# The first microseconds of a decoder-layer kernel: token loads, turns and the first two projection tiles in two token parts

## The reference, cut to what matters

```
z = h @ w_in                                    # h: 544 tokens x 1024, w_in: 1024 x 1696
q_lat, kv_lat, k_rope, lru_x, lru_gate = split(z)
xc, new_buf = causal_conv(lru_x, ...)           # width 4, depthwise
y, hT = rg_lru(xc, h0, lp)                      # sigmoid gates, exp, sqrt, a scan over tokens
mem_kv: m = rmsnorm(mem) ; k = m @ w_mem_k ; v = m @ w_mem_v     # 256 memory rows
```

## Time and profile before

| | |
|---|---|
| time, 3 runs | 1021.93, 1022.85, 1022.96 us; median 1022.85 |
| profiled execution, span from first to last instruction | 1026.9 us (no other time of that execution is given) |
| PE busy | 995.7 us, 97% |
| DVE, ACT, POOL busy | 518.6, 298.6, 447.6 us |
| chain that ended last | PE 82%, DVE 10%, POOL 3%, ACT 2% |
| mean granted TensorE clock | 0.989 |

### The profile page before, as it was taken

How to read it: one execution, slowest core, us unless ns; L and a number is a source line. 1 busy time by engine, 2 the same in 40 slices (tenths; PEclk the granted TensorE clock), 3 DMA queues, 4 the chain that set the end, 5 groups by cost and what they waited for, 6 DMA issues and landing times.

```text
span 1026.9 us, 19819 instructions
## 1 busy us (share of the span) xinstructions
PE 995.7 (97%) x8511; PEld 899.8 (88%) x8511; DVE 518.6 (51%) x731; ACT 298.6 (29%) x598; POOL 447.6 (44%) x284
## 2 busy tenths in 40 slices
PE   6999999998999999999999999999999999999998
PEld 5989898765677777999965799999999999999997
DVE  5789998478555555564155266421341134114413
ACT  6334265465444443121045122210120022002222
POOL 4545688500011112455320155555555555555551
PEclk8999999998999999999999999999999999999999
DMA  8323355514267772732193022233223322332222
GB/s 232 80 66 83 103 172 160 160 48 185 114 265 278 278 284 75 274 89 82 51 404 101 22 83 83 82 97 89 82 83 95 91 84 82 93 92 83 83 82 87
DMA packets 140556, 130.39 MB, mean 127 GB/s; under 512 B 13477, under 2 KB 133170, under 8 KB 136630
## 3 DMA queue, kind: packets, MB, share of 16 engines
q1 hardware_dynamic: 134888, 88.55, 28.6%
q0 software_dynamic: 2304, 37.75, 9.5%
q10 hardware_dynamic: 3278, 2.83, 0.8%
HBM read 123.53 MB, written 5.03 MB: 125 GB/s over the span
## 4 chain that ended last, share of the span: by engine, by line
PE 82%; DVE 10%; POOL 3%; ACT 2%; issue 2%; DMA 1%; ACTq 1%; SPq 0%; DVEq 0%; POOLq 0%
PE gps L582 56%; PE gps L942 5%; PE aux L956 3%; PE aux L983 3%; POOL wlo L521 2%; PE gps L1098 1%; PE gps L1180 1%; PE aux L962 1%; PE aux L894 1%; PE gps L1018 1%; DVE act_lo L1698 1%; PE gps L718 1%; PE aux L1111 1%; PE aux L973 1%; DVE lt L1782 1%
## 5 line engine op out<-in xcount | busy, mean ns | idle before, releaser
L582 PE MATMUL gps<-act_hi,whi 128*128 128x272 f32 x912 | 266.5, 292 | 5.7 <-POOL wlo L511 3.2
L497 POOL TENSOR_SCALAR whi<-wraw 128x1024 fp32r<-128x1024 f32 (+1 forms) x109 | 114.7, 1052 | 360.1 <-PE gps L582 300.0
L582 PE MATMUL gps<-act_lo,whi 128*128 128x272 f32 x912 | 265.0, 291 | 0.0
L582 PE MATMUL gps<-act_hi,wlo 128*128 128x272 f32 x912 | 264.6, 290 | 0.0
L500 POOL TENSOR_TENSOR wlo<-wraw,whi 128x1024 fp32r<-128x1024 f32 (+1 forms) x109 | 257.7, 2364 | 9.1
L582 PE MATMUL gps<-h_hi,whi 128*128 128x272 f32 x640 | 185.7, 290 | 0.0
L582 PE MATMUL gps<-h_lo,whi 128*128 128x272 f32 x640 | 185.1, 289 | 0.0
L582 PE MATMUL gps<-h_hi,wlo 128*128 128x272 f32 x640 | 184.6, 288 | 0.0
L582 PEld LDWEIGHTS gps<-act_hi,whi 128*128 128x128 f32 x912 | 173.2, 190 | 6.7 <-issue 3.7
L582 PEld LDWEIGHTS gps<-act_hi,wlo 128*128 128x128 f32 x912 | 173.1, 190 | 0.3 <-issue 0.2
L582 PEld LDWEIGHTS gps<-act_lo,whi 128*128 128x128 f32 x912 | 173.0, 190 | 0.0
(11 more groups left out here) (374 smaller groups left out, 1537.6 us busy)
## 6 DMA issues: line engine op xcount, KB each, us to landing
wraw<-in_w_up_dram SPq DMA_DIRECT2D x32, 512.0 KB, 4.0
wraw<-in_w_down_dram SPq DMA_DIRECT2D x32, 512.0 KB, 3.7
wraw<-in_w_in_dram SPq DMA_DIRECT2D x14, 512.0 KB, 4.2
kv<-in_cache_mem_k_dram SPq DMA_DIRECT2D x7, 1024.0 KB, 6.8
kv<-in_cache_mem_v_dram SPq DMA_DIRECT2D x7, 1024.0 KB, 14.0
wraw<-in_w_mem_k_dram SPq DMA_DIRECT2D x16, 256.0 KB, 2.9
wraw<-in_w_mem_v_dram SPq DMA_DIRECT2D x16, 256.0 KB, 3.3
wraw<-in_w_out_dram SPq DMA_DIRECT2D x8, 512.0 KB, 4.6
```

Of the source, the lines that this page charges most:

```text
L497: nc.gpsimd.tensor_scalar(whi[:, slot, 0:n], wraw[:, slot, 0:n], 1.0, 1.0, ALU.mult, ALU.mult).then_inc(pool_step, 1)
L582: mm = nc.tensor.matmul(out_of(a), w_of(w, k), x_of(x, k, part), start=(k == 0 and s == 0), stop=(k == k_tiles - 1 and s == 2))
```

## The change

- The tokens' loads and the weight units' are issued in another order: tokens 0 to 255, unit 0, tokens 256 to 511, the sample tokens, unit 1.
- Projection tiles 0 and 1 use token parts of 256 and 288 columns in place of 272 and 272, and are computed part by part: PE turns tokens 0 to 255, computes half of part 0 of tile 0, turns tokens 256 to 383, computes the other half, turns the rest, and so on. `act_hi` and `act_lo` are made in 8 + 8 instructions in place of 8 each.
- ACT makes `act_hi` of both parts before the squares of the token rows 128 to 543; before, the squares of rows 128 to 255 stood ahead of `act_hi`. A square root of one column at the very start loads its table.
- `dg` is made by DVE (two instructions) in place of POOL (five); the ones-matmul for the factors stands late in tile 1.
- PE turns the memory rows after tile 2 in place of after tile 1.

```
@@ sync
+            load_tokens(0)
+            load_tokens(1)
+            load_unit(0, win_v[:, :, IN_COLS[0]:IN_COLS[0] + 128], 1024)
+            load_tokens(2)
+            load_tokens(3)
+            sp.dma_start(xs[0:TS, 4, :], x_sample.rearrange("b t n -> (b t) n")).then_inc(x_in[4], 16)
+            load_unit(1, win_v[:, :, IN_COLS[1]:IN_COLS[1] + 128], 1024)
@@ gpsimd
-                if u == 2:
-                    pool.wait_ge(ident_in, 32)
-                    pool.wait_ge(nx_var, 3)
-                    for i in range(5):
...
-                        nc.gpsimd.tensor_scalar(dg[0:w, i, 0:w], ident[0:w, 0:w], rsx[0:w, i:i + 1], 1.0, ALU.mult,
@@ tensor
+            def token_factors():
+
+                pe.wait_ge(vec_ok, 3)
...
+            def first_part(t, a, ks):
+
+                for k in ks:
+                    if t == 0:
+                        pe.wait_ge(nx_lo, KD * a + k + 1)
+                        if a == 0 and k == KD // 2:
+                            pe.wait_ge(w_ready, 1)
...
+            token_turn(0)
+            token_turn(1)
+            pe.wait_ge(w_half, 1)
+            first_part(0, 0, range(4))
+            token_turn(2)
+            first_part(0, 0, range(4, 8))
+            token_turn(3)
+            token_turn(4)
+            first_part(0, 1, range(8)).then_inc(tile_done, 1)
             pe.wait_ge(xt_a, 5)
             pe.wait_ge(xt_d, 5)
...
+            head_turn()
+            pe.wait_ge(w_ready, 2)
+            first_part(1, 0, range(8))
+            first_part(1, 1, range(6))
+            token_factors()
+            first_part(1, 1, range(6, 8)).then_inc(tile_done, 1)
+
+            for i in range(2, 14):
+                act_tile(U_IN + i, T_IN + i)
+                if i == 2:
 
                     pe.wait_ge(vec_ok, 2)
                     pe.wait_ge(nx_var, 4)
                     pe.wait_ge(mn_d, 3)
@@ scalar
+            act.wait_ge(nx_var, 1)
+            nc.scalar.activation(nba[:, 7:8], rsx[:, 7:8], ACT.Sqrt)
+            token_copy(0)
+            row_square(0, 128)
+            token_copy(1)
             act.wait_ge(vec_ok, 1)
+            act.wait_ge(xt_a, 2)
+            early_hi(0, range(6))
+            token_copy(2)
+            early_hi(0, range(6, 8))
+            token_copy(3)
+            token_copy(4)
             act.wait_ge(xt_a, 5)
...
+            early_hi(1, range(8))
+            for i in range(1, 5):
                 row_square(i, 128 if i < 4 else TS)
@@ vector
+            early_lo(0, range(5))
+            token_copy(2)
+            early_lo(0, range(5, 8))
+            token_copy(3)
+            token_copy(4)
+            dve.wait_ge(xt_d, 5)
+            early_lo(1, range(8))
             dve.wait_ge(vec_T, 2)
             V.tensor_copy(vec[:, 8:NVEC], aux[:, 0, 8:NVEC])
...
+            V.tensor_tensor(dg[0:TS, 4, 0:TS], ident[0:TS, 0:TS], rsx[0:TS, 4:5].to_broadcast([TS, TS]), ALU.mult)
+            V.tensor_tensor(dg[:, 0:4, :], ident[:, :].unsqueeze(1).to_broadcast([128, 4, 128]),
+                            rsx[:, 0:4].unsqueeze(2).to_broadcast([128, 4, 128]), ALU.mult).then_inc(vec_ok, 1)
```

More of the change, by code:

```diff
@@ L645, in _, with token_turn @@
             nc.tensor.transpose(gps[:, 2, 0:8], vecrow[0:8, :], ident[0:8, 0:8]).then_inc(vec_T, 1)
-            for i in range(5):
+            def token_turn(i):
                 n = 128 if i < 4 else TS
@@ L656, in _ @@
                     mm.then_inc(xt_T, 1)
+            def token_factors():
+                pe.wait_ge(vec_ok, 3)
+                nc.tensor.matmul(aux[:, 2, 0:TP], ones[:, :], dg[:, 0:4, :].rearrange("p i n -> p (i n)"),
+                                 start=True, stop=True)
+                nc.tensor.matmul(aux[:, 3, 0:TS], ones[0:TS, :], dg[0:TS, 4, 0:TS], start=True, stop=True
+                                 ).then_inc(nx_ps, 1)
+            def first_part(t, a, ks):
[4 more added lines that the diff above has]
+                            pe.wait_ge(w_ready, 1)
+                    for s, (w, x) in enumerate(((0, 0), (1, 0), (0, 1))):
+                        mm = nc.tensor.matmul(gps[:, 2 * t + a, 0:EARLY_PARTS[a].stop - EARLY_PARTS[a].start],
+                                              weights(t, 128, w, k, 0, 128), (act_hi, act_lo)[x][:, k, EARLY_PARTS[a]],
+                                              start=(k == 0 and s == 0), stop=(k == KD - 1 and s == 2))
+                return mm
@@ L1266, in row_square, with token_copy @@
                                      ).then_inc(nx_sq, 1)
-            for i in range(5):
+            def token_copy(i):
                 n = 128 if i < 4 else TS
@@ L1682, in _, with token_copy @@
             V.memset(rsx[:, :], 1.0).then_inc(nx_var, 1)
-            for i in range(5):
+            def token_copy(i):
                 n = 128 if i < 4 else TS
-                if i == 0:
-                    dve.wait_ge(vec_T, 1)
-                    V.tensor_copy(vec[:, 0:8], gps[:, 2, 0:8]).then_inc(vec_ok, 1)
                 dve.wait_ge(xt_T, 2 * i + 2)
@@ L1709, in norm_inverse, with early_lo @@
                 V.reciprocal(rs, rs).then_inc(nm_var, 1)
[L1711 to L1719, removed]
+            def early_lo(a, ks):
+                for k in ks:
+                    dve.wait_ge(nx_hi, KD * a + k + 1)
+                    V.scalar_tensor_tensor(out=act_lo[:, k, EARLY_PARTS[a]], in0=XT[:, k, EARLY_PARTS[a]],
+                                           scalar=cols("norm_mix_g", k), in1=act_hi[:, k, EARLY_PARTS[a]].bitcast(F32),
+                                           op0=ALU.mult, op1=ALU.subtract).then_inc(nx_lo, 1)
+            early_lo(0, range(5))
[5 more added lines that the diff above has]
+            early_lo(1, range(8))
             dve.wait_ge(vec_T, 2)
```

61 lines of the change are left out of this document (31 added, 30 removed).

## The result

The changed kernel took 1039.96 us (median of 5, 1037.98 to 1045.21) against 1022.85; the ratio is 1.0153, 95% interval [1.0124, 1.0182]. Run again beside its variants it gave 1.0117 [1.0086, 1.0148]. The direction was forecast, the size was not: 9.2 us forecast, 15.6 us measured by the first ratio, outside the stated range, and 12.0 by the second, whose 1034.8 would lie inside it. The profiled execution was the slowest of the five: 1045.21 us, with a span of 1043.4.

A forecast was written before the change was run, and what follows sets the result against it. Bound by PE's tiles to 64.7 us, then DVE's recurrent branch: `conv(0)` 12.7 us later less 3.5 of slack delays tile 5's read-out 9.2 us, to 74.0; 1022.85 becomes 1032.0 us, range 1025.0 to 1036.5.

The forecast's parts named there:

- S1: End of `row_square(1)` on ACT, behind all sixteen `act_hi`; put at 25.8 us, bounds 17.9 and 27.5.
- from S1 to the memory rows squared: Load of the memory rows, 5.05 us to landing, then two squares of 2.3; S1 + 7.4.
- from there to `lru_in(0)` done: `nba`, root, scalings, table load, `spl`, `lru_in(0)`: 6.2 us as before, less 0.1 for waits; ends at S1 + 13.4, 39.2.
- tile 2 and the turn, to `conv(0)`: PE: tile 2 at 6.05 us, slow clock 1.7, turns 1.9, plus 0.1; `conv(0)` starts at 49.0 against 36.26.
- `conv(0)` to tile 5's read-out: DVE's own work of 24.8 us beside PE's mT_lo, gates, tiles 4 and 5; taken as 25 us.
- slack: DVE's idle between `conv(0)` and tile 5's read-out, 3.7 us, of which 3.5 was to absorb part of the delay.
- Unknown at `nba` and `spl`: POOL's splits of units 2 and 3 may fall on these small DVE steps: 0 to 2.4 us, taken as 0.
- the slow clock behind the long idle: PE's tile 2, behind 5 us of idle, at half speed for 3.4 us; loses 1.7 us.
- rival 2: Start is cut as the diff lays out and memory rows' chain hides; break-even S1 = 18.5; 1021 us; chance 0.08.
- the lock's term: DVE's small steps at `nba` and `spl` held by POOL's splits under the port lock: 0 to 2.4 us, taken as 0.
- its slow case: From `conv(0)` to tile 5's read-out, +26 us if idle ahead of the first gates brings the slow clock again.
- rival 3: Lock also hits `nba` and `spl`, and gates run slow: +2 and +1.5, so +12.7, 1035.5 us; chance 0.12.

The follow-up runs named there:

- b1: Kernel before with only PE's turn of the memory rows moved behind tile 2; ratio 1.0014 [0.9997, 1.0032] to the kernel before.
- a8: Changed kernel, memory rows turned ahead of tile 2, `row_square(1)` early, token turns ahead of matmuls, tiles 0 and 1 read out right behind `rs0`; ratio 0.9980.
- a2: Changed kernel with `row_square(1)` right behind ACT's copy of tokens 128 to 255; ratio 1.0096 to the kernel before.
- a4: Changed kernel with PE turning all tokens before the first matmul of tile 0; ratio 1.0081 to the kernel before.
- a5: Changed kernel with six extra 512-column matmuls on PE between tiles 1 and 2, into an unread bank; ratio 1.0138 to the kernel before.

## Why the direction was right and the size was not

Against the two profiles of the changed kernel (first, again), by the prediction's own steps:

| step | forecast | measured | off by |
|---|---|---|---|
| S1, end of `row_square(1)` | 25.8 | 27.4, 26.5 | +1.6, +0.7 |
| from S1 to the memory rows squared | 7.4 | 8.5, 7.8 | +1.1, +0.4 |
| from there to `lru_in(0)` done | 6.0 | 7.9, 7.9 | +1.9 |
| tile 2 and the turn, to `conv(0)` | 9.8 | 10.7, 11.0 | +0.9, +1.2 |
| `conv(0)` to tile 5's read-out | 25.0 | 26.6, 26.6 | +1.6 |
| tile 5 read | 74.0 | 81.1, 79.7 | +7.1, +5.7 |

- **Right**: the chain and each of its links (squares behind `act_hi`, load at 27.45 where 24 to 27 was said, idle of 6.8 us ahead of tile 2 ended by `lru_in(0)`, slow clock behind it, `conv(0)` late, slack used up); that `dg` on DVE is hidden in the changed kernel (ready at 32.6, used by PE at 34.8); that PE gains nothing in tiles 0 and 1 (tile 1 was in fact done 3 us later, at 37.1, which the same idle covers).
- **Wrong, first**: "Unknown at `nba` and `spl` ... 0 to 2.4 us ...; taken as 0". The steps of 0.24, 0.38 and 0.17 us took 0.48, 0.83 and 1.53. The middle one lay beside ACT's table load (DVE still waited 0.69 us for ACT behind it) and cost nothing; the other two add 1.6 us, and that is the whole difference between the 7.8 us from `nba` to the end of `lru_in(0)` here and the 6.2 of the kernel before. The other 0.3 of the 1.9 is hand-overs that the forecast left out. The units' loads stand behind the memory rows' on SP, so the splits that they feed run exactly when this chain does: it was no accident to be averaged, and the two changed profiles show the same 1.5 us. The nearest row, 1.79 against 0.77 in the earlier trace rows, said which end to take.
- **Wrong, second**: "gates and tile 5 at +24.4, or +26 if the idle ahead of the first gates brings the slow clock again. I take +25". Here it brought it, in both profiles of the changed kernel: 2.21 us of idle, then gates of 3.41 us (1.72 for the next ones). Of the seven profiles with this idle five have the slow clock behind it, and the 25.0 is what the other two show (24.9). I had the row for it, 1.72 us of idle and 3.4 us of slow clock, used it for tile 2 and not here.
- **Wrong, third**: S1 was put at 25.8 with PE's steps at nearly their full speed, the turns at 0.18 us each as the earlier trace rows gives them, a row at granted clock 1.00. In the first profile PE stood at 0.50 from 12 to 22 us. In the chain of waits the nine matmuls ahead of the last turns took 2.29 us there and 1.41 in the second profile, and the twelve turns behind them 2.09 and 1.25. `act_hi` of part 1 took 3.5 us in both, 0.44 an instruction where 0.40 was said. Beside it, the memory rows were there 6.2 and 5.4 us behind S1, where 5.05 had been read off; what makes that difference was not tested.
- **Wrong, fourth**: the slow clock behind the long idle was priced at 1.7 us, from the 3.4 us that it lasted behind the idle of 1.72. Behind idles of 6.8 and 6.0 us tile 2 took 8.7 and 9.0 us for 6.05, which is 2.6 and 3.0 more.
- Two readings in the prediction are off and change little. The `act_lo` at 13.41 ends at 15.20, 0.6 us behind POOL's instruction (14.61) and not with it: it waits for POOL and then does its own work. And rival 2's break-even comes to S1 = 18.9 with the 24.4 us that it uses, not 18.5.

S1 and the lock's term stayed within their bounds, the stretch from `conv(0)` came out 0.6 over the 26 of its slow case, and all five steps missed upwards. I had named rival 3 (+12.7) for the lock and the gates together and given it 0.12; it is what happened, with the slow clock of S1 and of tile 2 on top: +16.3 and +14.9 at the read-out. The profiled run of before also carried a slow stretch that cost it about 4.5 us (962.1 behind the read-out, b1 957.6), so that its span (4.05 above the median) was no neutral base, though the difference of the two spans was.

## What to carry to other kernels

When the first stages are reordered, follow the latest consumer of each engine's queue and not the stage that is meant to gain: here tile 0 was cut into parts, and a side chain (the memory rows' norm) that had 10 us of cover became the path through two other engines' orders. Here a newly exposed wait came with two companions, which are better priced with it at once than as rivals: the slow clock of PE behind its idle, and the engine that catches up on its work beside the exposed chain. An early read-out of the tile whose bank the next one needs was worth about as much as any of the other repairs, since its steps do not wait for POOL and the ones that it passes do.

## What the runs showed of the hardware

- The clock also dropped in a stretch with only short waits. Granted clock of PE in the kernel before, in the prompt's attention:

```profile
248.00:252.00 4.00, 2.45 (x12) 0.87 0.87 371
252.00:256.00 4.00, 4.00 (x18) 0.50 0.00 0
256.00:260.00 4.00, 4.00 (x18) 0.50 0.00 0
260.00:264.00 4.00, 3.90 (x40) 0.85 0.00 0
```

  PE had waited for ACT four times in the 12 us ahead of it, 0.39 to 1.55 us each. Six of sixteen profiles have such a stretch, some 10 us long, and a8's has a short one; in a2 and a4 PE was busy for the same 2.45 of 4 us at this place, and the clock stayed at 1.00. The spans behind tile 5 are 4.8 us longer with it in the mean. It fits the spread of the kernel before, 1021.3 to 1029.9 us over all sessions (that it makes the spread is not shown), which no comparison of two single profiles can see past.
- Idle of 2.2 us ahead of the first gates was followed by 0.50 (1.2 GHz) in five profiles and by the full clock in two (a2, a5), worth 1.6 us. The two profiles of the changed kernel, with equal instructions and the slow clock at this place both times, still read tile 5 1.4 us apart.
- The view's clock can't be trusted alone. In the second profile of the changed kernel it says 1.00 for 13 to 14 us, and the matmuls of 256 columns start 0.21 us apart, as they did at 0.50 in the first profile; at full speed it is 0.12:

```profile
13.00:14.00 1.00, 1.00 (x6) 1.00 (x6) 0.80 (x3) 0.00 (x0) 0.00 (x0) 1.00 1.25 176
```

```profile
13.47 0.41 PE L677 MATMUL gps<-act_hi,whi 128*128 128x256 f32 x1
13.69 0.41 PE L677 MATMUL gps<-act_hi,wlo 128*128 128x256 f32 x1
```

- The Trainium skill, "SBUF — State Buffer", section "Who interferes with whom", says that DVE and GpSimd share a pair of ports under an exclusive lock, and that of two instructions that need it the one that comes second blocks until the other is through. The traces agree down to the smallest steps: four columns took 1.53 us for 0.17, and 96 columns 2.22 for 0.22. In these rows the size of the DVE step says nothing of its cost beside POOL; which step it is does: the read-outs of 256 columns from PSUM kept their 0.42 us.
